# First RMSNorm from row sums, gate products between the tile transposes, in a two-layer decoder step

## What is computed

```
h    = rmsnorm(x, norm_w[0])                 # x * rsqrt(mean(x*x) + eps) * w, D_MODEL 2048
proj = h @ w_in                              # -> q,k,v (8192), z (4096), beta_raw, a_raw (64)
beta = sigmoid(beta_raw)
g    = -exp(a_log) * softplus(a_raw + dt_bias)
gc   = cumsum(g) in chunks of 64             # decays of the delta rule
```

## Time and profile before

| | us |
|---|---|
| runs | 2102.23, 2114.04, 2124.75; median 2114.04 |
| the profiled execution | 2103.39 |
| its span, first to last instruction | 2101.7 |
| busy: PE / DVE / ACT / POOL | 2062.8 / 1274.3 / 942.2 / 171.3 |

### The profile page before, as it was taken

One profiled execution on the slowest core, in us unless ns is written; L12 is line 12 of the kernel. 1 busy time (PEld: TensorE's weight loads), 2 busy tenths in 40 slices (PEclk: granted clock), 3 DMA queues, 4 the chain that ended last, 5 costly groups with the idle time before them and its releaser, 6 DMA issues.

```text
span 2101.7 us, 51659 instructions
## 1 busy us (share of the span) xinstructions
PE 2062.8 (98%) x19533; PEld 1971.3 (94%) x19533; DVE 1274.3 (61%) x2187; ACT 942.2 (45%) x2026; POOL 171.3 (8%) x320
## 2 busy tenths in 40 slices
PE   6999999999999999999999999999999999999998
PEld 3899999999999999999899999999999999999997
DVE  5567766766776776676754445554655656744444
ACT  3455555555555555555643344333333333433333
POOL 4011111011111101111100010000000000000010
PEclk9999999999999999999999999999999999999999
DMA  5545545345554545555445445544444445444442
GB/s 164 150 129 151 154 140 159 115 134 163 156 149 134 152 119 148 159 151 149 136 152 180 143 139 169 160 154 157 154 152 147 150 154 159 154 156 140 155 149 82
DMA packets 379977, 311.10 MB, mean 148 GB/s; under 512 B 19609, under 2 KB 375866, under 8 KB 379322
## 3 DMA queue, kind: packets, MB, share of 16 engines
q1 hardware_dynamic: 378042, 306.30, 48.2%
q10 hardware_dynamic: 1872, 3.96, 0.5%
HBM read 283.85 MB, written 27.25 MB: 148 GB/s over the span
## 4 chain that ended last, share of the span: by engine, by line
PE 97%; DVE 2%; issue 1%; DMA 0%; ACT 0%; SPq 0%; DVEq 0%; ACTq 0%
PE ps L295 28%; PE ps L296 27%; PE ps L297 27%; PE ps L1160 9%; PE ps L1319 2%; PE ps L1181 1%; DMA xtok<-in_x_sample_dram 0%; PE ps L1305 0%; DVE sq L851 0%; PE ps L1238 0%; PE ps L1282 0%; PE ps L1231 0%; DVE xlo L845 0%; PE ps L1287 0%; DVE wlo L286 0%
## 5 line engine op out<-in xcount | busy, mean ns | idle before, releaser
L295 PE MATMUL ps<-xhi,whi 128*128 128x320 f32 x3072 | 986.9, 321 | 4.8 <-DVE xlo L960 3.5
L297 PE MATMUL ps<-xhi,wlo 128*128 128x320 f32 x3072 | 950.2, 309 | 0.0
L296 PE MATMUL ps<-xlo,whi 128*128 128x320 f32 x3072 | 949.8, 309 | 0.0
L286 DVE TENSOR_TENSOR wlo<-wraw,whi 128x1024 fp32r<-128x1024 f32 (+1 forms) x484 | 582.0, 1224 | 239.1 <-ACT whi L281 236.5
L281 ACT ACTIVATE whi<-wraw 128x1024 fp32r<-128x1024 f32 (+1 forms) x484 | 495.6, 1049 | 263.1 <-PE ps L297 236.7
L295 PEld LDWEIGHTS ps<-xhi,whi 128*128 128x128 f32 x3072 | 578.2, 188 | 28.2 <-issue 20.8
L296 PEld LDWEIGHTS ps<-xlo,whi 128*128 128x128 f32 x3072 | 578.7, 188 | 0.9
L297 PEld LDWEIGHTS ps<-xhi,wlo 128*128 128x128 f32 x3072 | 577.7, 188 | 0.0
L296 PE MATMUL ps<-blo,whi 128*128 128x320 f32 x512 | 158.0, 309 | 0.0
L297 PE MATMUL ps<-bhi,wlo 128*128 128x320 f32 x512 | 158.0, 309 | 0.0
L295 PE MATMUL ps<-bhi,whi 128*128 128x320 f32 x512 | 157.9, 308 | 0.0
(11 more groups left out here) (338 smaller groups left out, 2104.0 us busy)
## 6 DMA issues: line engine op xcount, KB each, us to landing
wraw<-in_delta_w_in_dram SPq DMA_DIRECT2D x384, 256.0 KB, 3.2
wraw<-in_pool_w_in_dram SPq DMA_DIRECT2D x256, 256.0 KB, 3.0
wraw<-in_delta_w_out_dram SPq DMA_DIRECT2D x128, 256.0 KB, 3.3
wraw<-in_pool_w_out_dram SPq DMA_DIRECT2D x128, 256.0 KB, 3.2
s_s<-in_state_delta_dram SPq DMA_DIRECT2D x32, 512.0 KB, 6.2
out_dram<-s_s SPq DMA_DIRECT2D x32, 512.0 KB, 4.6
wraw<-in_pool_w_group_dram SPq DMA_DIRECT2D x64, 256.0 KB, 3.1
dec<-gc_rows SPq DMA_DIRECT2D x16, 320.0 KB, 5.1
```

Source lines behind the costliest of these rows:

```text
L286: nc.vector.tensor_tensor(wlo[:, slot, 0:width], wraw[:, slot, 0:width], whi[:, slot, 0:width].bitcast(F32), ALU.subtract).then_inc(E("w_l ...
L295: mm(o, whi[:, slot, w], hi[:, k_x, :], start=first, stop=False)
L296: mm(o, whi[:, slot, w], lo[:, k_x, :], start=False, stop=False)
L297: done = mm(o, wlo[:, slot, w], hi[:, k_x, :], start=False, stop=last)
```

## The change

The sums of squares are taken by ACT over the rows of `xtok` as each of the three loads lands (128, 128 and 64 tokens, 2048 values each, with an accumulator). The mean, root and reciprocal run on one value a partition; DVE multiplies the unit matrix by it (`diag`), and PE spreads it over the partitions with ones x diag. The copies of tiles 4 to 15 go into the loop over the scaling, the gate products of tile k-8 behind the transposes of tile k. PE runs 24 products on the unit matrix before x is there. `project(0, 0, 8)` starts right after the gate products; the gates' small PE products lie between its parts; ACT's and DVE's splits and the cache reads are reordered.

```diff
     rb = place(g, "rb", [T])
+    diag = branch[:, 24:26, :].rearrange("p k t -> p (k t)")
+    sq_x = branch[:, 0:20, :].rearrange("p k t -> p (k t)")
     vrow = place(g, "vrow", [P])
@@ -306,9 +308,9 @@
...
-        sp.dma_start(xtok[:, 0, :], x_prompt[0, 0:P, :]).then_inc(E("x_in"), 16)
-        sp.dma_start(xtok[:, 1, :], x_prompt[0, P:2 * P, :]).then_inc(E("x_in"), 16)
-        sp.dma_start(xtok[0:64, 2, :], x_sample.rearrange("b s c -> (b s) c")).then_inc(E("x_in"), 16)
+        sp.dma_start(xtok[:, 0, :], x_prompt[0, 0:P, :]).then_inc(E("x_in0"), 16)
+        sp.dma_start(xtok[:, 1, :], x_prompt[0, P:2 * P, :]).then_inc(E("x_in1"), 16)
+        sp.dma_start(xtok[0:64, 2, :], x_sample.rearrange("b s c -> (b s) c")).then_inc(E("x_in2"), 16)
@@ -553,27 +555,42 @@
...
 
-        for k in range(0, KT, 2):
+        def even_tile(k):
             act.wait_ge(E("tiles_t"), k + 1)
             sc.activation(ht[:, k, :], ps[:, 4 + k % 4, 0:T], ACT.Copy).then_inc(E("even_tiles"), 1)
-            if k >= 4:
-                act.wait_ge(E("sq_used"), k - 3)
-            act.wait_ge(E("even_tiles"), k // 2 + 1)
-            sc.activation(sq[:, k % 4, :], ht[:, k, :], ACT.Square).then_inc(E("sq_even"), 1)
-        act.wait_ge(E("odd_tiles"), KT // 2)
-        act.dma_start(ht_dram, ht[:].rearrange("p k t -> p (k t)")).then_inc(E("ht_saved"), 16)
+
+        act.wait_ge(E("consts"), 8)
+        sc.activation(small[:, 63:64], ones[:, 0:1], ACT.Sqrt)
+        for m, rows in enumerate((P, P, 64)):
+            act.wait_ge(E(f"x_in{m}"), 16)
+            sc.activation(sq_x[0:rows, DM * m:DM * m + DM], xtok[0:rows, m, :], ACT.Square,
+                          accum_out=small[0:rows, 3 + m:4 + m]).then_inc(E("sumsq"), 1)
+        even_tile(0)
         act.wait_ge(E("ms"), 1)
-        sc.activation(rb[:], rb[:], ACT.Sqrt).then_inc(E("rms"), 1)
-        for n in range(4):
-            split_hi(act, n, n, 512)
+        sc.activation(small[:, 6:8], small[:, 0:2], ACT.Sqrt)
+        sc.activation(small[0:64, 8:9], small[0:64, 2:3], ACT.Sqrt).then_inc(E("rms"), 1)
+        even_tile(2)
+        split_hi(act, 0, 0, 512)
         for k in range(KT):
+            if k % 2 == 0 and k + 4 < KT:
+                even_tile(k + 4)
+            if k in (2, 6, 10):
+                n = (k + 2) // 4
+                split_hi(act, n, n, 512)
+            if k == 12:
+                act.wait_ge(E("even_tiles"), KT // 2)
+                act.wait_ge(E("odd_tiles"), KT // 2)
+                act.dma_start(ht_dram, ht[:].rearrange("p k t -> p (k t)")).then_inc(E("ht_saved"), 16)
             act.wait_ge(E("xnorm"), k + 1)
             sc.activation(xhi[:, k, :], sq[:, k % 4, :], ACT.Copy).then_inc(E("x_hi"), 1)
-        split_hi(act, HEADS, 0)
-        split_hi(act, HEADS + 1, 1)
+            if k == 13:
+                split_hi(act, HEADS, 0)
+        for j in range(1, 4):
+            split_hi(act, HEADS + j, j)
 
         act.wait_ge(E("rows_in"), 128)
         sc.activation(gvec[:, 0, :], gvec[:, 0, :], ACT.Exp).then_inc(E("g_act"), 1)
+        split_hi(act, HEADS + 4, 0)
         act.wait_ge(E("g_in"), 3)
         sc.activation(gt[:], graw[:, :, 0:32], ACT.Tanh, scale=0.5).then_inc(E("g_act"), 1)
         act.wait_ge(E("g_in"), 4)
@@ -582,19 +599,14 @@
...
-        split_hi(act, HEADS + 4, 0)
         split_hi(act, HEADS + 5, 1)
-        split_hi(act, HEADS + 6, 2)
-        act.wait_ge(E("g_vec"), 7)
-        tv = table[:, :, 0:30].rearrange("p h (t u) -> p h t u", u=5)
-        sc.activation(tv[:, :, 4, :], tv[:, :, 0, :], ACT.Exp)
-        sc.activation(tv[:, :, 5, :], tv[:, :, 5, :], ACT.Exp)
-        sc.activation(table[:, :, EGL:EGL + 20], table[:, :, EGL:EGL + 20], ACT.Exp).then_inc(E("t_exp"), 1)
-        split_hi(act, HEADS + 7, 3)
-        act.wait_ge(E("g_vec"), 9)
-        act.dma_start(gc_dram, gcr[0:80, :]).then_inc(E("delta_out"), 16)
+
+        def first_exps():
+            act.wait_ge(E("g_vec"), 7)
+            tv = table[:, :, 0:30].rearrange("p h (t u) -> p h t u", u=5)
+            sc.activation(tv[:, :, 4, :], tv[:, :, 0, :], ACT.Exp)
+            sc.activation(tv[:, :, 5, :], tv[:, :, 5, :], ACT.Exp)
+            sc.activation(table[:, :, EGL:EGL + 20], table[:, :, EGL:EGL + 20], ACT.Exp).then_inc(E("t_exp"), 1)
 
         def loop_of(i):
             return not isinstance(i, int)
@@ -778,9 +790,14 @@
...
         qk_evac(0, HEADS + 4)
+        split_hi(act, HEADS + 6, 2)
         cc_evac(0)
-        for j in range(8, 10):
-            split_hi(act, HEADS + j, j % 4)
+        split_hi(act, HEADS + 7, 3)
+        first_exps()
+        split_hi(act, HEADS + 8, 0)
+        act.wait_ge(E("g_vec"), 9)
+        act.dma_start(gc_dram, gcr[0:80, :]).then_inc(E("delta_out"), 16)
+        split_hi(act, HEADS + 9, 1)
         v_evac(0, HEADS + 8)
@@ -815,30 +832,40 @@
...
 
-        for k in range(1, KT, 2):
+        def odd_tile(k):
             dve.wait_ge(E("tiles_t"), k + 1)
             v.tensor_copy(ht[:, k, :], ps[:, 4 + k % 4, 0:T]).then_inc(E("odd_tiles"), 1)
-            if k >= 4:
-                dve.wait_ge(E("sq_used"), k - 3)
-            dve.wait_ge(E("odd_tiles"), k // 2 + 1)
-            v.tensor_tensor(sq[:, k % 4, :], ht[:, k, :], ht[:, k, :], ALU.mult).then_inc(E("sq_odd"), 1)
+
+        odd_tile(1)
+        dve.wait_ge(E("sumsq"), 3)
+        v.tensor_scalar(small[:, 0:2], small[:, 3:5], 1.0 / DM, EPS, ALU.mult, ALU.add)
+        v.tensor_scalar(small[0:64, 2:3], small[0:64, 5:6], 1.0 / DM, EPS, ALU.mult, ALU.add).then_inc(E("ms"), 1)
+        dve.wait_ge(E("rms"), 1)
+        v.reciprocal(small[:, 9:11], small[:, 6:8])
+        v.reciprocal(small[0:64, 11:12], small[0:64, 8:9]).then_inc(E("rinv"), 1)
+        dve.wait_ge(E("rinv"), 1)
+        dve.wait_ge(E("ident"), 1)
+        for m, rows in enumerate((P, P, 64)):
+            last = v.tensor_scalar(diag[0:rows, P * m:P * m + rows], ident[0:rows, 0:rows], small[0:rows, 9 + m:10 + m], None,
+                                   ALU.mult)
+        last.then_inc(E("diag"), 1)
+        odd_tile(3)
         dve.wait_ge(E("vecs_ps"), 1)
         v.tensor_copy(vecs[:, 0:V_SCALE], ps[:, 1, 0:V_SCALE])
         v.tensor_scalar(vecs[:, V_SCALE:V_O + 1], ps[:, 1, V_SCALE:V_O + 1], 0.5, None, ALU.mult).then_inc(E("vecs"), 1)
-        cw = ps[:, 2, 0:256].rearrange("p (t n) -> p t n", t=TAPS)
-        for q in range(2):
-            v.tensor_copy(convw[:, :, q, :].rearrange("p h t -> p t h"), cw[:, :, NH * q:NH * q + NH])
-        for q in range(2):
-            last = v.tensor_copy(convw[:, :, 2 + q, :].rearrange("p h t -> p t h"),
-                                 cw[:, :, 2 * NH:4 * NH].rearrange("p t (h v) -> p t h v", v=2)[:, :, :, q])
-        last.then_inc(E("vecs"), 1)
-
-        dve.wait_ge(E("sq_used"), KT)
-        v.tensor_scalar(rb[:], ps[:, 0, 0:T], 1.0 / DM, EPS, ALU.mult, ALU.add).then_inc(E("ms"), 1)
-        dve.wait_ge(E("rms"), 1)
-        v.reciprocal(rb[:], rb[:]).then_inc(E("rinv"), 1)
-        dve.wait_ge(E("rinv"), 1)
+        dve.wait_ge(E("rb_ps"), 1)
+        v.tensor_copy(rb[:], ps[:, 0, 0:T]).then_inc(E("rb"), 1)
+        dve.wait_ge(E("rb"), 1)
         dve.wait_ge(E("vecs"), 1)
+
+        def conv_table():
+            cw = ps[:, 2, 0:256].rearrange("p (t n) -> p t n", t=TAPS)
+            for q in range(2):
+                v.tensor_copy(convw[:, :, q, :].rearrange("p h t -> p t h"), cw[:, :, NH * q:NH * q + NH])
+            for q in range(2):
+                last = v.tensor_copy(convw[:, :, 2 + q, :].rearrange("p h t -> p t h"),
+                                     cw[:, :, 2 * NH:4 * NH].rearrange("p t (h v) -> p t h v", v=2)[:, :, :, q])
+            last.then_inc(E("vecs"), 1)
 
         def low_x(k):
             dve.wait_ge(E("x_hi"), k + 1)
@@ -848,31 +875,35 @@
...
+            dve.wait_ge(E("odd_tiles" if k % 2 else "even_tiles"), k // 2 + 1)
             v.scalar_tensor_tensor(sq[:, k % 4, :], ht[:, k, :], vecs[:, k:k + 1], rb[:], ALU.mult, ALU.mult
                                    ).then_inc(E("xnorm"), 1)
-            if k == 1:
-                for n in range(4):
-                    split_lo(dve, n, n, 512)
+            if k % 2 == 0 and k + 5 < KT:
+                odd_tile(k + 5)
+            if k in (1, 3, 7, 11):
+                n = (k + 1) // 4
+                split_lo(dve, n, n, 512)
             if k >= 1:
                 low_x(k - 1)
+        split_lo(dve, HEADS, 0)
         low_x(KT - 1)
-        split_lo(dve, HEADS, 0)
+        conv_table()
         split_lo(dve, HEADS + 1, 1)
-
 
         dve.wait_ge(E("w_used"), 4)
         v.tensor_copy(gfeat[:], ps[:, 3, 0:T]).then_inc(E("g_in"), 1)
+        split_lo(dve, HEADS + 2, 2)
         dve.wait_ge(E("g_pe"), 1)
         gates = blocks(D0[:, 0:3 * P], 3)[:, :, 64:P]
         v.tensor_copy(graw[:, 0:2, :], gates[:, 0:2, :])
         v.tensor_copy(gtail[:], gates[:, 2, :]).then_inc(E("g_in"), 1)
+        split_lo(dve, HEADS + 3, 3)
         dve.wait_ge(E("g_pe"), 2)
```

(111 more changed lines are left out.)

## The result

Four executions of the changed kernel took 2230.0 to 2236.3 us, median 2232.1, beside 2102.2 to 2136.7, median 2119.4, of the kernel before. The ratio is 1.0585 with a 95% interval of 1.0545 to 1.0625. The forecast was 2094.5.

The account below looks back on a forecast made before the run. PE bounds 97% of the span, so only its start can gain: projection 20.9 us earlier, less 1.35 by k-tile 28, gives 19.5; from the median 2114.0 to 2094.5 us, range 2080 to 2108.

Parts of the forecast that it names:

- Y: Moment when k-tile 28 of head 0 begins; 87.7 us before, forecast 19.5 us earlier, order unchanged from there.
- Case C: Rounds lock into another phase, PE waiting for a split each round; at 2 us a round 2126 us; chance 0.04.
- the forecast's own signs of being wrong: S after 42, clock 0.5 between 14 and 30 us, `wlo` waits in rounds, or median moving under 10 us.
- A: PE stays at the low clock from its start into the loop; gain 14 us, 2100 us; chance 0.2.
- Squares: ACT's sums of squares over x rows: only the third counts, 2.0 us after x at 11.2, ending at 13.2.
- Mean to diag: Mean, root, reciprocal on one column and diag: 1.8 us, diag at 15.0; after spreading, first scaling at 16.8.
- PE's products ahead of x: 24 products on the unit matrix from 2.4 us, ending at 12.3; cost nothing unless the clock stays low.
- The loop: DVE's scaling, copies and splits: 20.1 us, plus 0.3 for ACT and 0.4 for POOL; PE's 1.0 a tile hidden.
- POOL beside the loop: POOL builds constants until 26 us beside DVE's loop, slowing its operations: 0.4 us, at most 3.0.
- From S to Y: First projection to k-tile 28: 28.7 us before, with changes of +0.75 - 1.3 + 1.6 + 0.3 = +1.35.
- S: Moment when project(0, 0, 8) begins: 59.00 us before, forecast 38.1, so 20.9 us earlier.
- The new wait for piece 7: PE waits in S to Y for DVE's split of piece 7, done after the `gct` copy: +1.6 us.

Follow-up runs that it names:

- products in the pause: Changed kernel with 6 products while PE waits for diag: with 23 at the start 2090.4 us, these plus DVE's reorder 2088.7, none at the start 2089.7.
- The run whose loop ends two instructions ahead of the edge: Changed kernel with 16 instead of 24 products on the unit matrix at PE's start: ratio 0.9941 to the kernel before, executions 2089.8 to 2114.3 us.

## Why the prediction was wrong

**The step that failed** is the sentence "Behind Y the pieces, the convolution and the rounds are in the same order, so nothing is given back or won". The order of the work was the same. What changed was the place of the code: 14 rounds took 10.2 us more each, where the forecast had nothing. An earlier step failed the same way: "So the row of products costs nothing unless the clock stays low." Its 8.6 us do lie in the wait for x; as code it cost 143.5 us. I counted instructions by their duration only; the instruction queue, with its 40 packets in the profile of before, was on the page I read and I drew nothing from it. Case C, slower, which had a chance of 0.04, had the direction, but neither the size (1.2 to 2 us a round against 10.2) nor the mechanism: `wlo` waits of 1.2 us do stand in the refetched rounds, but in the run without products they are gone with the packets (1.5 us in one wait, outside the rounds). Two of the forecast's own signs of being wrong showed: the clock of 0.5 between 14 and 30 us (A) and these waits (C). The change isn't the cause by anything it computes; 8 products in the kernel before did the same.

The loss by parts, from the changed kernel against the one without products: 65.2 + 17.7 + 2.2 us of waits for issue in the rounds, 19.7 - 1.5 for `wlo`, together 103. The other 40 or so are products at the low level behind the gaps: from k-tile 28 to the wait of 3.5 us for `xlo` behind the rounds PE did as many matmuls in both (11691), and of the 144.3 us that the stretch took longer it was busy for 42.4. First the changed kernel, then the run without products; clock in the third column from the right:

```profile
71.21:1160.89 1089.68, 986.44 (x11691) 909.75 (x11691) 667.99 (x1396) 512.42 (x1425) 123.86 (x156) 0.95 0.45 128
72.67:1018.07 945.40, 944.07 (x11691) 873.64 (x11691) 668.93 (x1396) 510.69 (x1425) 124.46 (x156) 1.00 0.50 145
```

**Point by point, the start.**
- Squares: 10.75 to 12.76, 2.0 us as summed. x was there 0.4 earlier. Right.
- Mean to diag: ended at 14.26, forecast 15.0. First scaling 16.52, forecast 16.8. Right.
- PE's products ahead of x: they ended at 11.0 (48 matmuls, 2.42 + 8.57) in place of 12.3; the high level was there by then (a transpose of the first tiles took 0.27, against 0.45 at the same place before). Right within the bounds.
- The loop: 24.4 us from the first scaling to the end of the last low part, against 20.1 + 0.3 + 0.4 = 20.8. Of the 3.6 us over it, 2.2 are two waits of DVE for PE's transposes (1.4 of them at 33.3), and 1.3 are the next point. The waits are the forecast's case A, which had a chance of 0.2: PE was at the low level, 1.8 us for a tile with its gate products (the third part of a tile's transposes came every 1.82 us; A had 1.75). I had taken the tile's cost, 1.0, from rows at the high level. With 24 and with 29 products the clock was low from 20 to 35 us; with products in the pause it read 0.78 to 1.00 from 20 to 25 us (three runs) and was low later. Without products the column shows 1.00 there, but a transpose took 0.42 us at 24.9: low too.
- POOL beside the loop: L872 took 561 ns in the mean and up to 997, L879 579 and up to 1000, against 487 and 548 before. 16 x 0.074 + 16 x 0.031 = 1.7 us, forecast 0.4, bound 3.0. The Trainium skill, SBUF — State Buffer, "SBUF: two separate sides", has DVE and GpSimd lock the shared port for a whole instruction. The trace agrees better with it than with the 0.19 of the row: two operations of DVE that began 0.2 us behind a POOL copy of 0.86 took 1.00 us, 0.5 more than their likes. No run took POOL's work away.

```profile
L872 DVE TENSOR_TENSOR xlo<-sq,xhi 128x320 fp32r<-128x320 f32 x16 | 9.0, 561 | 0.1
```

- From S to Y: 71.21 - 41.51 = 29.7, forecast 28.7 + 1.35 = 30.05. The new wait for piece 7 was summed at 1.6 and measured 1.51; the cache reads cost nothing.
- Y moved by 16.5 us where 19.5 were forecast, and the whole by 16.7 once the loop's place is taken out. The mechanism of the gain was right; the term that was mis-sized is the loop on DVE, 24.4 for 20.8, by the low level and the operations beside POOL.

The median of before that I carried the gain to, 2114, probably contained losses of the same kind; clear of the edge that kernel takes 2106. With the loop clear of it the changed kernel takes 2089.8 us, inside the forecast's range; but that a base 8 us too high and a gain 3 us too large partly cancel there is luck.

## What to carry to other kernels

Code ahead of a long loop is not free even where it runs in a wait: count how many blocks of 256 instructions the repeated part touches, before and after an edit, and pad or trim ahead of it. This case shows it for PE alone. The signs to look for are the instruction queue's packet count on the page and waits for "issue" once a round; a spread of the runs of 1% may be one (it went from 25 to 4 us when the loop was moved off the edge). Measure an edit with both kernels clear of such an edge, or the edit's own value can't be seen.

## What the runs showed of the hardware

- PE keeps seven blocks of 16 KB of its code over 14 repeats of a loop without a packet. With eight touched, packets came in nines: 72 or 126 over the 40, nine for each refetched round. The run whose loop ends two instructions ahead of the edge touches seven and had 36 more, nines as well. That eight blocks are the limit, and that a block fetched ahead is the one too many, would fit much of this but was not shown; it doesn't say why near the edge only some rounds are refetched.
- In the profiled executions 4 of 14 rounds were refetched with the loop's end two instructions ahead of the edge, 8 of 14 at one or two past it, all at 29 and 30 past. At two ahead the executions differ by chance (2089.8 to 2114.3 us); at two past they lie within 2144.3 to 2146.0.
- A refetched round costs 6.3 to 7.2 us when only four or eight are (the 6.3 from the kernel before with one product, (2152.2 - 2101.7) / 8), and 9.7 to 10.2 when all 14 are (the 9.7 from the kernel before with 8 products, (2240.3 - 2104.1) / 14).
- PE's clock stood at the low level (0.50) over 15.00 us in which PE was busy for 15.00 (20 to 35 us in the changed kernel), with transposes making up half of its matmuls, and at 1.00 over 19.00 us of a round in which it was busy for 19.00 (240 to 259 us).
